# Down weights of a mixture-of-experts stage loaded in runs of 16 KB, with h turned by quarter products

## The chip, the core and the metric

The kernel runs on one core of one Trainium2 chip. Its time is device time in microseconds, from three runs; beside it one execution was recorded by the hardware profiler, and all rows below come from that one. TensorE (PE) multiplies, VectorE (DVE), ScalarE (ACT) and GpSimd (POOL) do the rest, SyncE (SP) issues most of the DMAs, and 16 DMA engines move them.

## The reference

One decoder layer on 576 tokens of 1024 numbers (512 of a prompt, 64 of a sample group): a projection, sparse attention, a pooling branch, a merge, and then a mixture of 32 experts of which each token uses two. All is f32. The change lies in what an expert does, which in the reference is

```python
def run_block(args):
    tok, wt, e = args
    xb = xt[tok]
    hb = jax.nn.silu(xb @ w_exp_gate[e]) * (xb @ w_exp_up[e])
    return (hb @ w_exp_down[e]) * wt[:, None].astype(xb.dtype)
```

with gate and up weights of 1024 x 512 and down weights of 512 x 1024 for each expert, 2 MB each, 6 MB per expert and 201 MB for all 32.

## The kernel before, in words

The program is written by hand, engine by engine: each engine has its own list of instructions, and semaphores tie them together. There is no scheduler; the order on an engine is the order of the code. The layer up to the router takes the first half of the span. Then come the experts, each with a block of 64 token slots (CAP), and at the end the results are gathered and added per token. A second pass for experts with more than 64 tokens stands behind a branch on a flag.

There are two sets of buffers, s = 0 and 1, for even and odd experts; each holds gate (wg), up (wu) and down (wd) weights, 16 KB per partition each. `M[s]` holds the semaphores of a set. For expert n of a set:

- SP issues gate and up of the next expert of the set when the gate product has read them (`gu_done`), and down when the down product is done (`y_done`). All loads are on one queue and are moved in the order of issue. In a partition of wg and wu lie 8 rows of the weights that follow each other in memory, so a partition is one run of 16 KB. In a partition of wd lie 4 rows in two pairs (`by_half`): rows 2p and 2p+1, and rows 256+2p and 256+2p+1, two runs of 8 KB.
- PE multiplies x with gate and up (`gate_up`, 16 products of 512 columns, the two halves of the columns to the PSUM rows 0 to 63 and 64 to 127). Then it turns the x of the other set's next expert (`turn_x`), turns h (`turn_h`) and multiplies it with the down weights (`down`, 8 products of 512 columns).
- ACT applies silu to the gate half (line 1313), copies the turned x (1309) and the turned h (1317) to SBUF. DVE multiplies silu by up into hb (1647) and copies the result out (1651). POOL scatters y and gathers x by indirect DMAs on a queue of its own.

hb has the 64 tokens twice over the partitions: partitions 0 to 63 hold columns 0 to 255 of h and partitions 64 to 127 hold columns 256 to 511. The contraction of the down product runs over partitions, so h must be turned to match the rows of wd: a transpose of all 128 partitions at columns t, t+2, t+4, ... gives for each partition p the rows 2p+t (from the lower half) and 256+2p+t (from the upper half), each for 64 tokens. Two such transposes (t = 0 and 1) give all four.

The first experts are loaded in another order (lines 505 to 529): some weights lie in buffers of their own (wg2, wu2), so that much is in place before PE gets there. For the last expert gate and up come in two halves each (line 539).

Of the kernel before, what the change touches and what calls it, by code (L numbers as in the profile page):

```python
# [13 lines left out]
P = 128  # L14
# [20 lines left out]
NE = EG * EPG  # L35
DE = D // 2
KE = DE // P
CAP = 64
# [86 lines left out]
def program(nc, consts, where, x_prompt, x_sample, cache_k, cache_v, cache_idx_k, state_pool, page_table,  # L125
# [24 lines left out]
    with ctx:  # L150
# [9 lines left out]
        def at(off, *dims, rows=P):  # L160
            n = int(np.prod(dims))
            assert off + n <= AW, (off, dims)
            v = arena[0:rows, off:off + n]
            if len(dims) == 2:
                return v.rearrange("p (a b) -> p a b", b=dims[1])
            if len(dims) == 3:
                return v.rearrange("p (a b c) -> p a b c", b=dims[1], c=dims[2])
            return v
# [5 lines left out]
        def bank(b, n=512, rows=slice(0, P), at0=0):  # L174
            return psum[rows, b * 512 + at0:b * 512 + at0 + n]
# [27 lines left out]
        o = SMALL  # L203
# [23 lines left out]
        o = ZA + P * 9  # L227
# [6 lines left out]
        o = ZA  # L234
# [3 lines left out]
        o = PR  # L238
# [3 lines left out]
        o = PR  # L242
# [4 lines left out]
        o = ZB  # L247
# [32 lines left out]
        o = SMALL  # L280
# [3 lines left out]
        o = GAR + 4 * NT  # L284
# [19 lines left out]
        o = SG + 128  # L304
# [5 lines left out]
        o = SG  # L310
# [3 lines left out]
        xT = [at(o + s * 512, KD // 2, P) for s in range(2)]; o += 1024  # L314
        sg = [at(o + s * 512, DE // 2) for s in range(2)]; o += 1024
        hb = [at(o + s * 512, DE // 2) for s in range(2)]; o += 1024
        hT = [at(o + s * 256, KE // 2, P) for s in range(2)]; o += 512
        yo = [at(W1 - D + s * 512, 512) for s in range(2)]
        onehot = at(SG + 128 + 4 * D, TILES, 2, CAP)
        assert TILES * 2 * CAP <= D and 2 * CAP == P  # L320
# [9 lines left out]
        wd = [at(b + 8192, KE, D) for b in (W0, W1)]  # L330
# [12 lines left out]
        ident = const("ident")  # L343
# [26 lines left out]
        M = [{n: sem(f"{n}{s}") for n in  # L370
              ("wg_in wu_in wd_in xg_in xt_done xt_ev gu_done silu h_ready "
               "ht_done ht_ev y_done y_ev y_st").split()} for s in range(2)]

        OV, N0 = M[0], NE // 2
# [46 lines left out]
        def _(sp):  # L421
# [59 lines left out]

            g_v = w_exp_gate[0].rearrange("e (p k) n -> e p (k n)", k=KD)
            u_v = w_exp_up[0].rearrange("e (p k) n -> e p (k n)", k=KD)
            d_v = w_exp_down[0].rearrange("e (q p t) n -> e p q (t n)", q=2, t=KE // 2)

            def flat(t):
                return t.rearrange("p k n -> p (k n)")

            def by_half(t):
                return t.rearrange("p (q t) n -> p q (t n)", q=2)  # L490

            def load_expert(i, s, first=False, gate=True, up=True):
                e = 2 * i + s
                m = M[s]
                if up and not first:
                    sp.wait_ge(m["gu_done"], i)
                if gate:
                    sp.dma_start(flat(wg[s]), g_v[bass.ds(e, 1), :, :].squeeze(0)).then_inc(m["wg_in"], 16)
                if up:
                    sp.dma_start(flat(wu[s]), u_v[bass.ds(e, 1), :, :].squeeze(0)).then_inc(m["wu_in"], 16)  # L500
                if not first:
                    sp.wait_ge(m["y_done"], i)
                sp.dma_start(by_half(wd[s]), d_v[bass.ds(e, 1), :, :].squeeze(0)).then_inc(m["wd_in"], 16)

            load_expert(0, 0, first=True)
            load_ring(8)
# [6 lines left out]
            sp.dma_start(flat(wu[1]), u_v[1]).then_inc(M[1]["wu_in"], 16)  # L513
            sp.wait_ge(s_xst[0], 48)
            sp.wait_ge(s_xst[1], 32)
            sp.dma_start(by_half(wd[1]), d_v[1]).then_inc(M[1]["wd_in"], 16)
            sp.wait_ge(M[1]["xg_in"], 16)
            sp.dma_start(flat(wu2[0]), u_v[2, :, 0:4 * DE]).then_inc(S["part_in"], 16)
            sp.dma_start(flat(wu2[1]), u_v[2, :, 4 * DE:]).then_inc(M[0]["wu_in"], 16)
# [18 lines left out]
                for w, v, name in zip((wg[1], wu[1]), (g_v, u_v), names):  # L538
                    sp.dma_start(flat(w[:, ks, :]), v[NE - 1, :, 4 * half * DE:4 * (half + 1) * DE]).then_inc((M[1] if half else S)[name], 16)
            sp.wait_ge(M[1]["y_done"], NE // 2 - 1)  # L540
            sp.dma_start(by_half(wd[1]), d_v[NE - 1]).then_inc(M[1]["wd_in"], 16)

            sp.wait_ge(S["flag_ready"], 1)
            over = sp.value_load(flag[0:1, 0:1], min_val=0, max_val=NT)
            with sp.If(over > CAP):
                with sp.Fori(0, NE) as e:
                    sp.wait_ge(OV["y_done"], e * NB + N0)
                    sp.dma_start(flat(wg[0]), g_v[bass.ds(e, 1), :, :].squeeze(0)).then_inc(OV["wg_in"], 16)
                    sp.dma_start(flat(wu[0]), u_v[bass.ds(e, 1), :, :].squeeze(0)).then_inc(OV["wu_in"], 16)
                    sp.dma_start(by_half(wd[0]), d_v[bass.ds(e, 1), :, :].squeeze(0)).then_inc(OV["wd_in"], 16)  # L550
            with sp.Else():
                sp.nop()
            for i in range(TILES):
# [8 lines left out]
        def _(pe):  # L562
# [64 lines left out]
            for k in range(KD):  # L627
                last = pe.matmul(bank(6, HD), xnT[:, k, 0:P], wqi[:, k, NI * HD:NI * HD + HD], start=(k == 0), stop=(k == KD - 1))
# [158 lines left out]
            for u in range(U + 2):  # L787
                if u < U:
                    i, k = units[u]
# [232 lines left out]
            def turn_h(m, s, n):  # L1022
                pe.wait_ge(m["h_ready"], n + 1)
                pe.sem_inc(S["passed"], 1)
                for t in range(KE // 2):
                    last = pe.transpose(bank(1, P, at0=t * P), hb[s][:, t:KE // 2 * (P - 1) + t + 1:KE // 2], ident)  # L1026
                last.then_inc(m["ht_done"], 1)

            def down(m, s, n):
                pe.wait_ge(m["ht_ev"], n + 1)  # L1030
                for k in range(KE):
                    for half in range(2):
                        last = pe.matmul(bank(4 + s, 512, slice(64 * half, 64 * half + 64)), hT[s][:, k % 2, CAP * (k // 2):CAP * (k // 2) + CAP],  # L1033
                                         wd[s][:, k, 512 * half:512 * half + 512],
                                         start=(k == 0), stop=(k == KE - 1))
                last.then_inc(m["y_done"], 1)
# [900 lines left out]
```

## Time and profile before

| | us |
|---|---|
| median of three timed runs | 1116.12 (1114.67 to 1117.65) |
| the profiled execution | 1115.16 |
| its span, first to last instruction | 1113.5 |
| PE busy | 944.4 (85%) |
| mean granted clock of TensorE | 0.951 |
| gate and up products, line 1018 | 238.9 busy, 992 instructions |
| down products, line 1033 | 116.9 busy, 512 instructions |
| a down load, issue to landing | 22.9 (median of 32) |

Slices are fortieths of the span, 27.8 us each. PEclk is the clock granted to TensorE, as a share of 2.4 GHz; 0.50 is 1.2 GHz. PE's busy time is not work at its peak: its instructions overlap, so the time from the first start to the last end of a group says more than their mean. The DMA share is the busy share of the 16 engines; as packets of an engine overlap a little, it can stand slightly above 1. "issue" in the chain is a piece in which the engine waited for nothing that the profile names.

### The profile page before, as it was taken

To read this page: it belongs to the slowest core of one execution; us is meant where nothing else is said; L and a number is where in the kernel's file an instruction comes from. 1 tells how busy PE (TensorE), PEld (TensorE's weight loads), DVE (VectorE), ACT (ScalarE), POOL (GpSimd) and SP (SyncE) were. 2 spreads that over 40 slices of the span, in tenths; PEclk is the share of its full clock that TensorE was granted. 3 is DMA by queue.
4 is the path that set the end of the run, shared out by engine and by line. 5 is a ranking of instruction groups with operands and counts; after the bars stand their busy time and mean duration, and the time that the engine had idled before them with its cause. 6 is when DMAs were issued, how large, how long until landed. Compare 5 with 4: busy or idle time off the path is not lost.

```text
span 1113.5 us, 11556 instructions
## 1 busy us (share of the span) xinstructions
PE 944.4 (85%) x4412; PEld 510.2 (46%) x4412; DVE 338.7 (30%) x743; ACT 201.7 (18%) x445; POOL 198.3 (18%) x296
## 2 busy tenths in 40 slices
PE   7978999999999998999976998788778887887770
PEld 6633444767776566774543433333233333333220
DVE  2269999973331111330143100000000000000006
ACT  3243111213344233000121000000000000000012
POOL 2730650100001200000231121111110111011113
PEclk9989999999999999999996999999999999899995
DMA  9920221610204527913035999999999999999937
GB/s 335 392 78 1 76 85 38 231 39 38 76 1 152 203 100 216 378 64 150 38 126 227 408 419 426 421 424 425 426 423 424 424 425 425 421 425 425 422 136 252
DMA packets 51814, 283.72 MB, mean 255 GB/s; under 512 B 8476, under 2 KB 9344, under 8 KB 32823
## 3 DMA queue, kind: packets, MB, share of 16 engines
q1 hardware_dynamic: 40935, 246.21, 55.0%
q0 software_dynamic: 10784, 36.97, 9.2%
q8 instruction: 25, 0.41, 0.2%
q14 instruction: 14, 0.11, 0.0%
q10 hardware_dynamic: 56, 0.01, 0.0%
HBM read 267.38 MB, written 23.17 MB: 261 GB/s over the span
## 4 chain that ended last, share of the span: by engine, by line
PE 64%; DVE 18%; issue 7%; ACT 4%; DMA 3%; SPq 2%; POOL 1%; ACTq 0%; POOLq 0%; DVEq 0%
PE psum L1018 21%; PE psum L1033 11%; PE psum L780 9%; DVE arena L1421 6%; DVE arena L1419 6%; PE psum L934 5%; PE psum L916 3%; PE psum L604 3%; DMA arena<-in_w_branch_pool 2%; PE psum L1026 1%; PE psum L868 1%; DVE arena L1647 1%; ACT arena L1313 1%; ACT arena L1317 1%; PE psum L834 1%
## 5 line engine op out<-in xcount | busy, mean ns | idle before, releaser
L1018 PE MATMUL psum<-arena 128*64 128x512 f32 x992 | 238.9, 637 | 56.5 <-issue 55.6
L1018 PEld LDWEIGHTS psum<-arena 128*64 128x64 f32 x992 | 86.2, 147 | 207.5 <-issue 207.5
L1033 PE MATMUL psum<-arena 128*64 128x512 f32 x512 | 116.9, 597 | 17.7 <-ACT arena L1317 17.7
L780 PE MATMUL psum<-arena 128*128 128x288 f32 x480 | 126.1, 416 | 0.0
L780 PEld LDWEIGHTS psum<-arena 128*128 128x128 f32 x480 | 89.6, 192 | 31.0 <-issue 8.1
L1647 DVE TENSOR_TENSOR arena<-arena,psum 128x256 f32<-128x256 f32 x32 | 13.5, 421 | 292.1 <-ACT arena L1313 292.1
L1313 ACT ACTIVATE arena<-psum 128x256 f32<-128x256 f32 x32 | 12.3, 384 | 418.1 <-PE psum L1018 407.3
L590 PE MATMUL psum<-arena 128*128 128x512 f32 x192 | 86.2, 604 | 2.1 <-ACT arena L1184 2.1
L1033 PEld LDWEIGHTS psum<-arena 128*64 128x64 f32 x512 | 40.4, 136 | 72.1 <-issue 72.1
L1651 DVE COPY arena<-psum 128x512 f32<-128x512 f32 x32 | 22.1, 691 | 157.1 <-PE psum L1033 157.1
L916 PE MATMUL psum<-arena 128*128 128x288 f32 x256 | 64.3, 415 | 3.7 <-DMA arena<-in_w_branch_pool 3.7
L1419 DVE MAX8 arena<-arena 64x8 f32<-64x1032 f32 (+3 forms) x80 | 66.2, 828 | 2.8
L1845 POOL CAST arena<-arena 128x1 int32 x30 | 5.6, 185 | 329.7 <-DVE arena L1651 329.7
L1421 DVE MATCH_REPLACE8 arena<-arena 64x1032 f32<-64x1032 f32 (+3 forms) x76 | 61.9, 814 | 0.0
L916 PEld LDWEIGHTS psum<-arena 128*128 128x128 f32 x256 | 49.5, 194 | 18.5 <-DMA arena<-in_w_branch_pool 4.6
L590 PEld LDWEIGHTS psum<-arena 128*128 128x128 f32 x192 | 36.3, 193 | 45.1 <-issue 42.8
L934 PE MATMUL psum<-arena 128*128 128x512 f32 x128 | 55.8, 593 | 1.1 <-issue 1.1
L1091 ACT COPY arena<-psum 128x512 f32<-128x512 f32 (+6 forms) x106 | 47.0, 490 | 53.8 <-PE psum L807 31.8
L1701 POOL DMA_INDIRECT arena<-xn_d,arena x32 | 33.4, 1043 | 33.8 <-POOL arena L1839 25.9
L1705 POOL DMA_INDIRECT y_d<-arena x32 | 33.2, 1037 | 29.0 <-POOL arena L1845 27.4
L934 PEld LDWEIGHTS psum<-arena 128*128 128x128 f32 x128 | 23.9, 190 | 29.7 <-issue 29.7
L1821 POOL TENSOR_TENSOR arena<-arena 128x1024 f32<-128x1024 f32 (+1 forms) x5 | 11.7, 2344 | 139.0 <-ACT arena L1301 139.0
(263 smaller groups left out, 930.8 us busy)
## 6 DMA issues: line engine op xcount, KB each, us to landing
arena<-in_w_exp_down SPq DMA_DIRECT2D x32, 2048.0 KB, 22.9
arena<-in_w_exp_gate SPq DMA_DIRECT2D x31, 2048.0 KB, 18.2
arena<-in_w_exp_up SPq DMA_DIRECT2D x30, 2048.0 KB, 22.6
arena<-in_w_in SPq DMA_DIRECT2D x7, 2048.0 KB, 8.6
y_d<-arena SPq DMA_DIRECT2D x1, 8192.0 KB
arena<-in_x_prompt SPq DMA_DIRECT2D x8, 512.0 KB, 7.2
arena<-in_w_out SPq DMA_DIRECT2D x2, 2048.0 KB, 10.4
arena<-in_w_exp_up SPq DMA_DIRECT2D x4, 1024.0 KB, 12.8
```

Of the source, the lines that this page charges most:

```text
L590: last = pe.matmul(bank(b, n, slice(0, r)), lhs, w[:, k, 0:n], start=(k == 0), stop=(k == KD - 1))
L604: last = pe.matmul(out, lhs, wqi[:, k, QIH * half:QIH * half + QIH], start=(k == 0), stop=(k == KD - 1))
L780: last = pe.matmul(bank(2 + n % 2 if n < SAMPLE_G else 2, HN), ring[slot % 2][:, k, m * P:(m + 1) * P], xnT[:, k, HN * hh:HN * hh + HN], s ...
L916: last = pe.matmul(bank(b, HN), w[:, 4 * br + k, m * P:(m + 1) * P], src[:, k, tc], start=(k == 0), stop=(k == 3))
L934: last = pe.matmul(bank(4 + 2 * (i % 2) + half), sgA[k][:, i * P:(i + 1) * P], ring[(R_OUT + half) % 2][:, k, :], start=(k == 0), stop=(k ...
L1018: last = pe.matmul(bank(2 + s, 512, rows).rearrange("p (w n) -> p w n", w=2), x_k, wgu[s][:, :, DE * k + 256 * q:DE * k + 256 * q + 256], ...
L1033: last = pe.matmul(bank(4 + s, 512, slice(64 * half, 64 * half + 64)), hT[s][:, k % 2, CAP * (k // 2):CAP * (k // 2) + CAP], wd[s][:, k, 5 ...
L1091: last = act.copy(out, src(b))
L1419: link(dve.max(m8, src))
L1421: link(dve.match_replace(w, m8, src, LOW))
L1701: pool.indirect_dma_start(xg[s], None, xn2_d, bass.IndirectOffsetOnAxis(ap=sidx[s], axis=0), bounds_check=2 * NT - 1, oob_is_err=False).th ...
L1705: pool.indirect_dma_start(y_halves, bass.IndirectOffsetOnAxis(ap=syid[s], axis=0), yo[s], None, bounds_check=2 * FIRST - 1, oob_is_err=Fal ...
```

## The change

The down weights are loaded as `wg` and `wu` are: partition p gets rows 4p to 4p+3, one run of 16 KB. For h to match, partition p of the turned h must hold columns 4p to 4p+3. Partitions 0 to 63 of it come from the lower half of hb alone and partitions 64 to 127 from the upper half alone, so for each of the four t there are two products with a 64x64 part of the identity: the lower quarter of the array for the lower half, and the upper for the upper. They are plain f32 products in place of transposes, all into bank 1. `hT` has the same size, ordered by t. ACT's copy and the number of down products stay.

```diff
--- before.py
+++ after.py
@@ -314,7 +314,7 @@
         xT = [at(o + s * 512, KD // 2, P) for s in range(2)]; o += 1024
         sg = [at(o + s * 512, DE // 2) for s in range(2)]; o += 1024
         hb = [at(o + s * 512, DE // 2) for s in range(2)]; o += 1024
-        hT = [at(o + s * 256, KE // 2, P) for s in range(2)]; o += 512
+        hT = [at(o + s * 256, KE, CAP) for s in range(2)]; o += 512
         yo = [at(W1 - D + s * 512, 512) for s in range(2)]
         onehot = at(SG + 128 + 4 * D, TILES, 2, CAP)
         assert TILES * 2 * CAP <= D and 2 * CAP == P
@@ -481,13 +481,10 @@
 
             g_v = w_exp_gate[0].rearrange("e (p k) n -> e p (k n)", k=KD)
             u_v = w_exp_up[0].rearrange("e (p k) n -> e p (k n)", k=KD)
-            d_v = w_exp_down[0].rearrange("e (q p t) n -> e p q (t n)", q=2, t=KE // 2)
+            d_v = w_exp_down[0].rearrange("e (p t) n -> e p (t n)", t=KE)
 
             def flat(t):
                 return t.rearrange("p k n -> p (k n)")
-
-            def by_half(t):
-                return t.rearrange("p (q t) n -> p q (t n)", q=2)
 
             def load_expert(i, s, first=False, gate=True, up=True):
                 e = 2 * i + s
@@ -500,7 +497,7 @@
                     sp.dma_start(flat(wu[s]), u_v[bass.ds(e, 1), :, :].squeeze(0)).then_inc(m["wu_in"], 16)
                 if not first:
                     sp.wait_ge(m["y_done"], i)
-                sp.dma_start(by_half(wd[s]), d_v[bass.ds(e, 1), :, :].squeeze(0)).then_inc(m["wd_in"], 16)
+                sp.dma_start(flat(wd[s]), d_v[bass.ds(e, 1), :, :].squeeze(0)).then_inc(m["wd_in"], 16)
 
             load_expert(0, 0, first=True)
             load_ring(8)
@@ -513,7 +510,7 @@
             sp.dma_start(flat(wu[1]), u_v[1]).then_inc(M[1]["wu_in"], 16)
             sp.wait_ge(s_xst[0], 48)
             sp.wait_ge(s_xst[1], 32)
-            sp.dma_start(by_half(wd[1]), d_v[1]).then_inc(M[1]["wd_in"], 16)
+            sp.dma_start(flat(wd[1]), d_v[1]).then_inc(M[1]["wd_in"], 16)
             sp.wait_ge(M[1]["xg_in"], 16)
             sp.dma_start(flat(wu2[0]), u_v[2, :, 0:4 * DE]).then_inc(S["part_in"], 16)
             sp.dma_start(flat(wu2[1]), u_v[2, :, 4 * DE:]).then_inc(M[0]["wu_in"], 16)
@@ -538,7 +535,7 @@
                 for w, v, name in zip((wg[1], wu[1]), (g_v, u_v), names):
                     sp.dma_start(flat(w[:, ks, :]), v[NE - 1, :, 4 * half * DE:4 * (half + 1) * DE]).then_inc((M[1] if half else S)[name], 16)
             sp.wait_ge(M[1]["y_done"], NE // 2 - 1)
-            sp.dma_start(by_half(wd[1]), d_v[NE - 1]).then_inc(M[1]["wd_in"], 16)
+            sp.dma_start(flat(wd[1]), d_v[NE - 1]).then_inc(M[1]["wd_in"], 16)
 
             sp.wait_ge(S["flag_ready"], 1)
             over = sp.value_load(flag[0:1, 0:1], min_val=0, max_val=NT)
@@ -547,7 +544,7 @@
                     sp.wait_ge(OV["y_done"], e * NB + N0)
                     sp.dma_start(flat(wg[0]), g_v[bass.ds(e, 1), :, :].squeeze(0)).then_inc(OV["wg_in"], 16)
                     sp.dma_start(flat(wu[0]), u_v[bass.ds(e, 1), :, :].squeeze(0)).then_inc(OV["wu_in"], 16)
-                    sp.dma_start(by_half(wd[0]), d_v[bass.ds(e, 1), :, :].squeeze(0)).then_inc(OV["wd_in"], 16)
+                    sp.dma_start(flat(wd[0]), d_v[bass.ds(e, 1), :, :].squeeze(0)).then_inc(OV["wd_in"], 16)
             with sp.Else():
                 sp.nop()
             for i in range(TILES):
@@ -1022,15 +1019,17 @@
             def turn_h(m, s, n):
                 pe.wait_ge(m["h_ready"], n + 1)
                 pe.sem_inc(S["passed"], 1)
-                for t in range(KE // 2):
-                    last = pe.transpose(bank(1, P, at0=t * P), hb[s][:, t:KE // 2 * (P - 1) + t + 1:KE // 2], ident)
+                for t in range(KE):
+                    for q in range(2):
+                        rows = slice(CAP * q, CAP * q + CAP)
+                        last = pe.matmul(bank(1, CAP, rows, t * CAP), hb[s][rows, t:KE * (CAP - 1) + t + 1:KE], ident[rows, rows], start=True, stop=True)
                 last.then_inc(m["ht_done"], 1)
 
             def down(m, s, n):
                 pe.wait_ge(m["ht_ev"], n + 1)
                 for k in range(KE):
                     for half in range(2):
-                        last = pe.matmul(bank(4 + s, 512, slice(64 * half, 64 * half + 64)), hT[s][:, k % 2, CAP * (k // 2):CAP * (k // 2) + CAP],
+                        last = pe.matmul(bank(4 + s, 512, slice(64 * half, 64 * half + 64)), hT[s][:, k, :],
                                          wd[s][:, k, 512 * half:512 * half + 512],
                                          start=(k == 0), stop=(k == KE - 1))
                 last.then_inc(m["y_done"], 1)
```

The order of instructions on PE does not change, only what stands in a turn. At the end of the program, in the last pair of experts (the rows are the gate product, the turn of x, the turn of h, the down product, and for the last expert the same without a turn of x), before:

```order
L1018 MATMUL psum<-arena 64x512 x16
L1001 MATMUL psum<-arena 128x128 x4
L1026 MATMUL psum<-arena 128x128 x2
L1033 MATMUL psum<-arena 64x512 x8
L1018 MATMUL psum<-arena 64x512 x16
L1026 MATMUL psum<-arena 128x128 x2
L1033 MATMUL psum<-arena 64x512 x8
```

and in the changed kernel, at the same place:

```order
L1015 MATMUL psum<-arena 64x512 x16
L998 MATMUL psum<-arena 128x128 x4
L1025 MATMUL psum<-arena 64x64 x8
L1032 MATMUL psum<-arena 64x512 x8
L1015 MATMUL psum<-arena 64x512 x16
L1025 MATMUL psum<-arena 64x64 x8
L1032 MATMUL psum<-arena 64x512 x8
```

Two products of 128x128 are now eight of 64x64 between the same neighbours. On SP, at the start of the expert stage (up of expert 2 in two halves, gate of 4, down of 2, up of 4, gate and up of 3, down of 3 and 4), before:

```order
L518 DMA arena<-in_w_exp_up 128x2048
L519 DMA arena<-in_w_exp_up 128x2048
L523 DMA arena<-in_w_exp_gate 128x4096
L503 DMA arena<-in_w_exp_down 128x2x2048
L526 DMA arena<-in_w_exp_up 128x4096
L498 DMA arena<-in_w_exp_gate 128x4096
L500 DMA arena<-in_w_exp_up 128x4096
L503 DMA arena<-in_w_exp_down 128x2x2048 x2
```

and now:

```order
L515 DMA arena<-in_w_exp_up 128x2048
L516 DMA arena<-in_w_exp_up 128x2048
L520 DMA arena<-in_w_exp_gate 128x4096
L500 DMA arena<-in_w_exp_down 128x4096
L523 DMA arena<-in_w_exp_up 128x4096
L495 DMA arena<-in_w_exp_gate 128x4096
L497 DMA arena<-in_w_exp_up 128x4096
L500 DMA arena<-in_w_exp_down 128x4096 x2
```

No load has moved; each down load has one run per partition where it had two.

## Rows read from the trace of the kernel before

**Rows 1.** The page: what the DMA engines moved in 40 slices, and SP's queue.
```profile
GB/s 335 392 78 1 76 85 38 231 39 38 76 1 152 203 100 216 378 64 150 38 126 227 408 419 426 421 424 425 426 423 424 424 425 425 421 425 425 422 136 252
...
q1 hardware_dynamic: 40935, 246.21, 55.0%
```

**Rows 2.** Windows: us, busy PE PEld DVE ACT POOL, clock, DMA share, GB/s.
```profile
600.00:640.00 40.00, 37.24 (x200) 18.08 (x198) 3.34 (x6) 4.03 (x9) 5.29 (x10) 0.97 0.87 356
1000.00:1040.00 40.00, 30.34 (x134) 11.62 (x132) 2.91 (x5) 2.69 (x6) 7.39 (x12) 0.96 1.02 427
```

**Rows 3.** The chain that ended last: start us, us, what.
```profile
637.66 6.88 PE psum L1018 x32
...
675.36 6.88 PE psum L1018 x32
...
687.92 2.65 issue
690.58 8.80 PE psum L1018 x32
...
1050.30 2.67 issue
1052.97 8.69 PE psum L1018 x32
1063.69 3.65 PE psum L1033 x16
1067.34 6.88 PE psum L1018 x32
```

**Rows 4.** Issue to landing of up(30), down(4), gate(4) and down(1), in this order.
```profile
DMA to landing us min/median/max: 23.7/23.7/23.7
...
DMA to landing us min/median/max: 10.8/10.8/10.8
...
DMA to landing us min/median/max: 8.7/8.7/8.7
...
DMA to landing us min/median/max: 7.4/7.4/7.4
```

**Rows 5.** SP's queue, windows 502:506, 585.5:589, 609.2:612.8: packets, MB, share of 16 engines.
```profile
q1 hardware_dynamic: 775, 1.59, 103.0%
...
q1 hardware_dynamic: 182, 1.49, 101.2%
...
q1 hardware_dynamic: 94, 1.54, 99.7%
```

**Rows 6.** The chain again, ahead of the branch products.
```profile
447.32 21.12 DMA arena<-in_w_branch_pool
```

**Rows 7.** Timeline of PE, an expert's turn of h: start us, us, instructions.
```profile
1015.11 0.48 PE L1026 MATMUL psum<-arena 128*128 128x128 f32 x2 [0.34 <-DVE arena L1647]
```

**Rows 8.** Timeline of PE, small f32 products earlier in the program.
```profile
27.37 2.00 PE L616 MATMUL psum<-arena 64*128 64x64 f32 x16
...
330.03 1.09 PE L818 MATMUL psum<-arena 128*64 128x128 f32 x16
...
332.07 1.97 PE L818 MATMUL psum<-arena 128*64 128x128 f32 x32
```

**Rows 9.** The chain, products of 512 columns on the full width.
```profile
529.45 6.87 PE psum L934 x16
```

**Rows 10.** Timeline of SP, and one window, at the start of the experts.
```profile
612.49 0.38 SPq L503 DMA_DIRECT2D arena<-in_w_exp_down  x1
...
625.05 13.01 SPq L503 DMA_DIRECT2D arena<-in_w_exp_down  x2
644.55 0.34 SPq L498 DMA_DIRECT2D arena<-in_w_exp_gate  x1
...
613.00:614.00 1.00, 1.00 (x7) 0.37 (x5) 0.19 (x1) 0.00 (x0) 0.19 (x1) 1.00 0.56 131
```

**Rows 11.** Window at the start of expert 30's gate product; columns as in rows 2.
```profile
1053.00:1056.00 3.00, 3.00 (x8) 1.05 (x10) 0.00 (x0) 0.00 (x0) 0.41 (x1) 0.50 1.02 423
```

## The prediction

> **What bounds the kernel now.** I read the page first, then the windows by stretch, the chain, SP's queue, and last the few places where PE turns a tile. On the page the reader is to see that the core moves 419 to 426 GB/s in slices 24 to 38 [rows 1]: this is the stage of the 32 experts, from 597 to 1080 us, and the change touches nothing else. The windows say what that means: from 1000 to 1040 us the DMA share is 1.02 while PE is busy for 30.3 of 40 us; from 600 to 640 PE is busy for 37.2 and DMA stands at 0.87 [rows 2]. The chain shows the two regimes that follow. Experts 3 to 6 start 12.57 us apart (637.66 to 675.36, three steps) with nothing idle before them; experts 7 to 30 start 15.76 us apart (690.58 to 1052.97, 23 steps), most of them after a piece called "issue", a wait for weights, of 1.3 to 3.3 us; the first of these and the last are shown [rows 3]. So PE works off a lead, and then the loads set the pace. The last such wait stands before expert 30. Its up weights were issued at 1029.2 and landed 23.7 us later [rows 4], at 1052.9, and the gate and up products start at 1052.97 [rows 3]. From there to 1080 PE works without a wait for a load: two turns of h and two down products lie in that stretch. The end of the program is the landing of up(30), plus PE's tail, plus 33 us of combining that stay as they are.
>
> **The down loads.** A down load was 256 runs of 8 KB and becomes 128 runs of 16 KB, as gate and up have, so each of 16 engines handles 8 packets fewer per expert. What does a packet cost beside its bytes? In 4.0 us in which only 2 KB packets move, 775 of them carry 1.59 MB, 397 GB/s, or 82.5 ns each on 16 engines; in 3.5 us of down load alone, 182 packets of 8 KB carry 1.49 MB, 426 GB/s, 307.7 ns each [rows 5]. The 6144 B between them cost 225.2 ns, so 2048 B cost 75.1, and 7.4 ns are left for the packet. Eight packets: 0.059 us per expert. That counts where the down load stands ahead of one that is waited for: down(2) to down(29), 28 loads in the full queue ahead of up(30), and down(0), which SP issues ahead of the branch weights on which the chain waits until 468.5 [rows 6]. 29 x 0.059 = 1.7 us less. Above it stands the packets' own time: 182 packets fill 101.2% of 3.5 us, 311.4 ns each, 94 packets of 16 KB fill 99.7% of 3.6 us, 610.9 ns each [rows 5]; twice the first less the second is 11.9 ns, and 29 x 8 x 11.9 ns = 2.8 us. The rates of the same two windows, 426 and 428 GB/s, give only 0.7 us, and the overhead may be hidden altogether. Below nothing: started on an empty queue, gate(4) in 16 KB runs took 8.7 us to land and down(1) in 8 KB runs 7.4 [rows 4]; if long runs start slower, down(2), the only one near an empty queue, loses up to 1.3 us once. I take 1.7, which lies in the middle and rests on two pure windows of wall time.
>
> The Trainium skill (DMA: Bandwidth & Descriptors, section Why small descriptors are slow) gives a packet a fixed overhead of about 3 cycles beside one per 32 bytes. By that a down load would gain 0.6% of its 4.92 us, 0.8 us over 29 loads where my rows give 1.7, and the sum below would be +1.0 instead of +0.1. The rates 426 and 428 fit that rule better; the 2 KB window fits it worse.
>
> **The turn of h.** Two transposes of 128x128 stand there now, 0.48 us from first start to last end [rows 7]. In their place come eight products. They are f32 products and no transposes, and each f32 product shows as two instructions (the 8 calls at line 1033 are 16 in a row), so 16 instructions with 64x64 stationary and 64 moving columns. No such row exists. Nearest is line 818, 64 stationary and 128 moving columns: 16 instructions in 1.09 us, 32 in 1.97, 0.055 us each [rows 8]. I take 1.09 us, that is D = +0.61 us per expert. From above: line 616, 64 moving columns under 128 stationary ones, 16 in 2.00 us, D = +1.5 [rows 8]. From below: two column halves do run beside each other, as 16 instructions of 512 columns take 3.65 us at line 1033 and 6.87 at line 934 over the full width [rows 3, 9]; if the two quarters of a slice did the same, 16 would take 0.27 + 15 x 0.0275 = 0.68 us, D = +0.2. ACT copies the same 128x256 as before, and the down products again read 64 columns in a row.
>
> **Where D counts.** (a) In the tail, for experts 30 and 31: 2D = +1.2 us. Expert 31's weights bring no new wait, since there is none now (1063.69 + 3.65 = 1067.34 [rows 3]) and PE only gets later. (b) At the start: SP issues down(2) when expert 0's down product is done, at 612.49, with up(4) behind it; the queue had run dry, 131 GB/s from 613 to 614 [rows 10]. The whole D = +0.6 us goes on the load chain. (c) A little later gate(5) is issued at 644.55 by the gate product of expert 3, three turns down the chain; down(4), ahead of it, was issued at 637.69, the second of the two in the row at 625.05, and landed 10.8 us later, at 648.5 [rows 4, 10]. A load needs some 2 us from issue to full rate (the 131 GB/s stand 0.5 to 1.5 us behind down(2)), so there are 3.9 - 2 = 1.9 us of room against 3D - D = 2D = 1.2: enough, up to D = 0.95. (d) In experts 7 to 29 D lies in the wait of 1.3 to 3.3 us for weights. That cover is gone if D passes 15.76 - 12.57 = 3.2 us.
>
> **The sum.** +0.6 (opening) +1.2 (tail) -1.7 (loads) = +0.1 us. The profiled execution took 1115.16 us around its span of 1113.5, so it would be 1115.3; the three timed runs have a median of 1116.12, 0.96 more, and I forecast 1116.2 us. Less than 0.3%, or 3.3 us, can't be told from no change here.
>
> **Rivals.**
> *R1, the packets hide.* Nothing comes back from longer runs and only 3D is left: +1.8 us, 1117.9. For it: 426 and 428 GB/s. Against it: 397 with 2 KB packets, and 311.4 ns twice against 610.9 once [rows 5].
> *R2, faster by the clock.* Expert 30's products came after 2.67 us of idle with the granted clock at 0.50 for their first 3 us, 1.2 GHz, and took 8.69 us where expert 31's took 6.88 at full clock [rows 3, 11]. Over experts 7 to 30, all five waits of 1.3 to 1.9 us were followed by 7.1 us, and of the fifteen of 2.6 us or more ten by 8.4 to 10.0. The change makes PE busier, so that the wait before expert 30 shrinks by some 0.7 to 2.0 us. If the clock then stays at 2.4 GHz, the tail is 1.8 us shorter: 1114.4; with D = 0.2 and 2.8 for the loads it is 1112.1. Against it: a wait between 1.9 and 2.6 us never occurs, so no row tells which way it goes.
> *R3, slower: the quarters don't overlap and the array drains between them.* Both write bank 1, one from rows 0 to 63 and one from rows 64 to 127; where the kernel now has products from both row halves (line 712), they go to two banks. At line 616's 2.00 us D is 1.5: 3 x 1.5, plus 2 x 1.5 - 1.9 = 1.1 us of dry queue at gate(5), less 1.7 = +3.9 us, 1120.0. The opening decides from D = 0.95. If each of the 16 ran its whole 0.28 us alone, D would be 4.0, past the 3.2 of cover: PE would be the bound, 32 x 16.6 us where the stage takes 483, +47 us.
> The Trainium skill (TensorEngine Tiling, Restrictions and Gotchas) says that different row tiles can't access one PSUM bank at the same time, and under Key Properties that a change of tiling mode drains the engine. By that rule something of R3 must come; no row of before has two row tiles on one bank.
> *R4, the change doesn't do what it says*: the runs are cut to 8 KB all the same, +1.8 us. Gate loads do move in 16 KB packets, 94 for 1.54 MB [rows 5], which speaks against it.
>
> **Chances.** Forecast 0.50 (0.46 within 0.3%, 0.02 faster, 0.02 slower); R1 0.16 (0.14 within, 0.02 slower); R2 0.18 (0.14 faster, 0.04 within, as it needs help from D or the loads to pass 3.3 us); R3 0.12 (slower); R4 0.04 (within). Faster 0.16, same 0.68, slower 0.16. The forecast's own range is 1114 to 1118.5; with R1, R2 and the near form of R3 it becomes 1112.0 to 1120.5.
>
> **What would show it.** Queue q1 should carry 4096 packets fewer than 40935 [rows 1]. Each turn should hold 16 instructions in 1.1 us. The waits before experts 7 to 29 should be shorter by about 0.7 us and their spacing 15.70 us (15.76 if R1 holds). down(2) should be issued 0.6 us later. From 1052.97 to the last down product there are 27.0 us; there should be 28.2, or 26.4 at full clock. I am wrong if the spacing moves by more than 0.15 us either way, if the turn takes over 1.5 us, or if the queue runs dry after 640.

## The result and the profile after

| | before | changed |
|---|---|---|
| median of 20 runs, us | 1115.45 (1114.18 to 1117.84) | 1118.45 (1114.0 to 1124.31) |
| ratio to before | | 1.0024 (1.0015 to 1.0033) |
| span of the profiled execution | 1113.5 | 1115.6 |
| SP's queue, packets | 40935 | 36839 |

The changed kernel is 0.24% slower, 2.7 us by the ratio (3.0 by the medians): below the 0.3% that was called "the same" and inside the range, though 0.05 us from the upper end of the forecast's own range of 1114 to 1118.5. It is off the forecast of +0.1 us and clear of noise with this many runs.

The page of the changed kernel shows that the change does what it says: 4096 packets fewer on SP's queue for the same bytes [rows 1], and 512 small instructions, 16 per expert (8 products, each shown as two).

```profile
GB/s 328 390 85 0 76 59 62 207 49 52 76 1 148 195 112 204 370 82 151 38 123 211 404 399 427 425 424 427 427 425 427 427 425 428 424 427 427 422 140 249
...
q1 hardware_dynamic: 36839, 246.21, 54.8%
...
L1025 PE MATMUL psum<-arena 64*64 64x64 f32 x512 | 37.5, 284 | 11.7 <-DVE arena L1646 11.7
```

In the full part of the stage it moves 424 to 428 GB/s where 421 to 426 stood. The chain of the changed kernel (start, us, what) answers to [rows 3]:

```profile
599.19 9.85 PE psum L1015 x32
...
709.89 7.10 PE psum L1015 x32
...
1052.89 1.88 issue
1054.77 7.10 PE psum L1015 x32
1064.60 3.65 PE psum L1032 x16
1068.25 6.88 PE psum L1015 x32
1077.87 3.67 PE psum L1032 x16
```

Expert 8 starts at 709.89 and expert 30 at 1054.77, 22 steps of 15.68 us. In before expert 30 starts at 1052.97 [rows 3] and expert 8 at 706.05 (the row below), steps of 15.77 us:

```profile
706.05 7.10 PE psum L1018 x32
```

So the loads did get faster, by 0.09 us per expert in this pair of traces. One turn, in the timeline of PE (before: [rows 7]):

```profile
1017.38 1.17 PE L1025 MATMUL psum<-arena 64*64 64x64 f32 x16 [0.34 <-DVE arena L1646]
```

With the copy behind it that shifts the down product by 0.70 us (from the start of the turn to the start of the down product it is 1.73 us, and 1.03 before). The prediction had put this D, the extra time of a turn, at 0.61.

The span of one execution can't carry a verdict of 2 us. Expert 0's gate product starts at 599.19 here and at 597.03 before, and in the twelve further traces below it starts anywhere from 596.07 to 599.98, although nothing ahead of it differs in a way that goes with that. And expert 0's gate product itself takes 8.5 to 9.9 us by how soon the clock comes up. I therefore read three numbers from every trace: **M**, from the end of expert 0's gate product to the start of expert 30's; **G**, expert 30's gate product (7.10 us at full clock, 8.5 to 8.8 where it starts at half of it); and **T**, from the start of that product to the end of the last down product, without G.

| kernel | M | G | T |
|---|---|---|---|
| before | 446.28 | 8.69 | 18.27 |
| changed | 445.73 | 7.10 | 19.67 |

M is 0.55 us shorter and T 1.40 us longer, which gives +0.9 us. G is 1.6 us shorter, which would turn the sum to -0.7. The timing says +2.7, so one trace of each doesn't account for the time.

How far can one trace be trusted? M is fixed by the loads and by the turns in the opening. Three kernels of this document have the loads and the opening of before: their M is 446.28, 446.04 and 446.32. Three traces have those of the changed kernel, one of them with the products of the turn in another form: 445.73, 445.60 and 446.09. So M scatters by 0.3 to 0.5 us, and the changed kernel is 0.4 us shorter in the mean (445.81 against 446.21). T repeats to 0.02 us, but for the clock of the last down product. G is partly chance and partly the change itself, as the section on the clock shows.

The last row is one of the prediction's own signs of being wrong. In the windows of the changed kernel (us; busy PE, PEld, DVE, ACT, POOL; clock, DMA share, GB/s) the queue runs dry behind 640 us:

```profile
649.00:651.00 2.00, 1.66 (x20) 1.50 (x20) 0.42 (x1) 0.97 (x2) 0.00 (x0) 1.00 0.81 221
```

Before, at the same distance from expert 0's gate product:

```profile
646.70:648.70 2.00, 2.00 (x10) 0.76 (x11) 0.00 (x0) 0.00 (x0) 0.00 (x0) 1.00 1.01 428
```

### The profile page after: what moved, and what is told of

Its sections match the earlier page's. It is cut to its first block, busy times and chain, and to the rows that moved or that the text cites. A ratio compares the mean times of both kernels' runs of the same rounds, so it can differ in the third digit from the quotient of the medians.

```text
span 1115.6 us, 12452 instructions
## 1 busy us (share of the span) xinstructions
PE 961.2 (86%) x4860; PEld 534.2 (48%) x4860; DVE 338.9 (30%) x743; ACT 201.7 (18%) x445; POOL 199.3 (18%) x296
## 3 DMA queue, kind: packets, MB, share of 16 engines
q1 hardware_dynamic: 36839, 246.21, 54.8%
## 4 chain that ended last, share of the span: by engine, by line
PE 65%; DVE 18%; issue 6%; ACT 5%; DMA 3%; SPq 2%; POOL 0%; ACTq 0%; POOLq 0%; DVEq 0%
PE psum L1015 21%; PE psum L1032 10%; PE psum L777 9%; DVE arena L1420 6%; DVE arena L1418 6%; PE psum L931 5%; PE psum L1025 3%; PE psum L913 3%; PE psum L601 3%; DMA arena<-in_w_branch_pool 2%; PE psum L865 1%; DVE arena L1646 1%; ACT arena L1312 1%; ACT arena L1316 1%; PE psum L613 1%
## 5 line engine op out<-in xcount | busy, mean ns | idle before, releaser
L1015 PE MATMUL psum<-arena 128*64 128x512 f32 x992 | 232.3, 622 | 40.4 <-issue 39.6
L1032 PE MATMUL psum<-arena 128*64 128x512 f32 x512 | 116.9, 597 | 17.7 <-ACT arena L1316 17.7
L777 PEld LDWEIGHTS psum<-arena 128*128 128x128 f32 x480 | 89.6, 192 | 31.0 <-issue 8.1
L913 PEld LDWEIGHTS psum<-arena 128*128 128x128 f32 x256 | 49.5, 194 | 19.3 <-DMA arena<-in_w_branch_pool 5.4
L587 PEld LDWEIGHTS psum<-arena 128*128 128x128 f32 x192 | 36.2, 193 | 45.1 <-issue 42.8
L1025 PE MATMUL psum<-arena 64*64 64x64 f32 x512 | 37.5, 284 | 11.7 <-DVE arena L1646 11.7
L1025 PEld LDWEIGHTS psum<-arena 64*64 64x64 f32 x512 | 34.0, 210 | 17.6 <-issue 17.6
```

The costliest lines, as they stand in the source:

```text
L587: last = pe.matmul(bank(b, n, slice(0, r)), lhs, w[:, k, 0:n], start=(k == 0), stop=(k == KD - 1))
L777: last = pe.matmul(bank(2 + n % 2 if n < SAMPLE_G else 2, HN), ring[slot % 2][:, k, m * P:(m + 1) * P], xnT[:, k, HN * hh:HN * hh + HN], s ...
L913: last = pe.matmul(bank(b, HN), w[:, 4 * br + k, m * P:(m + 1) * P], src[:, k, tc], start=(k == 0), stop=(k == 3))
L1015: last = pe.matmul(bank(2 + s, 512, rows).rearrange("p (w n) -> p w n", w=2), x_k, wgu[s][:, :, DE * k + 256 * q:DE * k + 256 * q + 256], ...
L1025: last = pe.matmul(bank(1, CAP, rows, t * CAP), hb[s][rows, t:KE * (CAP - 1) + t + 1:KE], ident[rows, rows], start=True, stop=True)
```

## The experiments

The theory was that the loads gain a little, and that the longer turn costs in the opening and in the tail alone. The rivals: long runs are part of the loss; the turn costs all along the stage; the form of the quarter products is what makes the turn long.

**Each half of the change alone.** `e1_loads_only` has the new loads and the old turn; `e2_turn_only` the old loads and the new turn. They leave out that h must match the rows of wd, so their outputs are not those of the layer, but the amount of work on each engine is. The same holds below wherever the turn changes without the loads. The diff is the part on the turn of the first kernel against the changed one; the second has the same lines the other way, against the kernel before. In both, `hT` and the index of the down product go with the turn.

```diff
-                for t in range(KE):
-                    for q in range(2):
-                        rows = slice(CAP * q, CAP * q + CAP)
-                        last = pe.matmul(bank(1, CAP, rows, t * CAP), hb[s][rows, t:KE * (CAP - 1) + t + 1:KE], ident[rows, rows], start=True, stop=True)
+                for t in range(KE // 2):
+                    last = pe.transpose(bank(1, P, at0=t * P), hb[s][:, t:KE // 2 * (P - 1) + t + 1:KE // 2], ident)
```

> Down loads in 16 KB runs, but h turned by the two old transposes, so h does not match the rows of wd (the down product sums other pairs than the reference). Theory A (loads gain a little, the longer turn costs in opening, dry queue and tail): the load gain stands alone, spacing of experts 15.68 us, about 1.8 us faster than before (ratio 0.998). Rival B (long runs cost somewhere, for example at the start of a burst or for the branch weights, and are part of the loss): not faster than before, ratio 1.000 to 1.002.

> Down loads in 8 KB runs as before, but h turned by the eight quarter products, so h does not match the rows of wd. Theory A: the longer turn (+0.70 us) costs in the opening (0.9), in a dry queue before expert 5's gate load (about 1.2) and in the tail (1.4): +3.5 to +4.5 us, ratio 1.003 to 1.004, spacing of experts in the load-bound part 15.76 us as before. Rival B: +1.5 us or less, since the loads' part of the loss is absent.

Measured: loads alone 0.9982 (0.9968 to 0.9996), 2.0 us faster; turn alone 1.0038 (1.0022 to 1.0054), 4.2 us slower. Both as theory A had them, and rival B is gone: the longer runs gain and are no part of the loss. The spacing of experts 8 to 30 is 15.68 to 15.70 us in all six traces with 16 KB runs in the middle (that of the pairs below, with another gate product, left aside), and 15.75 to 15.78 in the seven with 8 KB runs. In the traces M is 444.25 with the loads alone (-2.0) and 448.49 with the turn alone (+2.2), T is 18.28 and 21.37. The T of the second holds 1.4 us of turns and 1.7 us that nobody had expected: the last down product took 5.37 us for 3.65 (below).

**Where the turn costs.** Old loads throughout; the quarter products stand in some experts only, chosen in `turn_h` by the number n of the pair: one of these three returns, for experts 0 to 3, for 30 and 31, and for 4 to 29 (`overflow` is set only for the second pass, which keeps the old turn).

```diff
+            def quarters(n):
+                return isinstance(n, int) and n in (0, 1) and not overflow[0]
...
+                return isinstance(n, int) and n == NE // 2 - 1 and not overflow[0]
...
+                return not (isinstance(n, int) and n in (0, 1, NE // 2 - 1)) and not overflow[0]
```

> All loads as before; quarter products in experts 0 to 3 only, whose h then does not match wd. Theory A: opening 0.7 to 0.9 us and a dry queue before gate(5) of about 1.2 us, +2 us, ratio 1.0018. Rival F: less than +0.8 us, the loss being spread over all experts.

> All loads as before; quarter products in experts 30 and 31 only, whose h then does not match wd. Theory A: 2 x 0.70 = +1.4 us, ratio 1.0013, all behind the landing of up(30). Rival F: +0.3 us or less.

> All loads as before; quarter products in experts 4 to 29 only, whose h then does not match wd. Theory A: no change (ratio 1.000, within 0.6 us), since PE waits 1.3 to 3.3 us for weights there; the waits shrink by 0.7 us. Rival F: most of the +4.2 us of the kernel with the turn alone shows here, ratio 1.002 or more.

| turn in experts | ratio | M | G | T |
|---|---|---|---|---|
| 0 to 3 | 1.0033 (1.0019 to 1.0047) | 448.51 | 8.80 | 18.27 |
| 30, 31 | 1.0014 (1.0000 to 1.0029) | 446.04 | 8.55 | 19.66 |
| 4 to 29 | 0.9991 (0.9979 to 1.0003) | 446.32 | 7.10 | 18.28 |
| all 32 | 1.0038 (1.0022 to 1.0054) | 448.49 | 7.10 | 21.37 |

The six experts at the ends pay everything, and 26 turns of 0.70 us in the middle pay nothing. M says it well inside its scatter: +2.23 with the turn in experts 0 to 3, +2.21 with it in all, +0.04 with it in 4 to 29. By time the first kernel is 3.7 us slower where theory A had +2, its interval just above it; the trace gives 2.2, and the rest is not explained. The interval of the second kernel holds rival F's +0.3 us too; T, 1.39 longer, decides it. In the middle the wait for weights takes it up. From 695 to 1053 us PE's waits for weights (total, times, longest) were, before:

```profile
PE psum L1018 <- issue: 53.0, 22, 3.3
```

and with the turn in experts 4 to 29:

```profile
PE psum L1019 <- issue: 37.3, 23, 2.5
```

15.7 us less waiting for some 16 us of turns in that window. Rival F is refuted.

**Inside the opening.** The turn in expert 0 only, and in experts 1 and 2 only (one return each).

```diff
+            def quarters(n, s):
+                return isinstance(n, int) and n == 0 and s == 0 and not overflow[0]
...
+                return isinstance(n, int) and 2 * n + s in (1, 2) and not overflow[0]
```

> All loads as before; quarter products in expert 0 only, whose h then does not match wd. Theory A (two separate places in the opening): down(2) is issued 0.70 us later on a dry queue and everything behind it shifts, expert 30's gate product starts 0.7 us later behind expert 0's gate product than before (446.3 us); gate(5) and the queue ahead of it are late alike, so it brings nothing more. Rival G (the whole +2.2 us of the opening comes from down(2)): +2.2 us. In time +0.7 against +2.2 us, which the timing can hardly tell; the trace can.

> All loads as before; quarter products in experts 1 and 2 only, whose h then does not match wd. Theory A: down(2) is issued as before, gate(5) 1.4 us later on a queue that has almost run dry (dip to about 250 GB/s for two us at 40 us behind expert 0's gate product), expert 30 starts 1.3 to 1.5 us later than before. Rival G: down(2) is all, no shift. Rival H (gate(5) has the 1.9 us of room that the prediction gave it from the landing of down(4)): no shift and no dip.

Expert 0 alone: 1.0005 (0.9996 to 1.0014), M = 446.98, +0.70. Experts 1 and 2: 1.0022 (1.0008 to 1.0036), M = 447.22, +0.94. So there are two places, as A had it, though it had put the second at 1.3 to 1.5 us, and H, the 1.9 us of room for gate(5) of the prediction, is wrong. SP's queue in the kernel with the turn in experts 1 and 2 (timeline; the row with x2 holds down(3) and down(4)), and the window behind gate(5):

```profile
613.17 0.38 SPq L504 DMA_DIRECT2D arena<-in_w_exp_down  x1
...
626.44 13.71 SPq L504 DMA_DIRECT2D arena<-in_w_exp_down  x2
646.63 0.34 SPq L499 DMA_DIRECT2D arena<-in_w_exp_gate  x1
```
```profile
647.00:649.00 2.00, 1.11 (x7) 0.63 (x7) 0.42 (x1) 0.98 (x3) 0.00 (x0) 1.00 0.93 260
```

down(2) is issued 5.8 us behind expert 0's gate product, as in before; gate(5) comes 1.4 us later than there, and at once the rate is 260 GB/s for two us.

Why is there no room? A landing is the end of the slowest of 16 engines, and the traces keep the time at which each of the 16 counted its share of down(4) as done. In before the first was done at 646.05, the last at 648.51 (the landing that the prediction used), the mean is 646.98. gate(5) was issued at 644.55, so the first engine was through with everything ahead of it 1.5 us later and the mean one 2.4 us later, where the landing stands 3.9 us behind. Less the prediction's own 2 us of start, 0.4 us of room are left in place of 1.9, and a delay of 1.4 us costs 1.0 by that estimate; 0.94 was measured. With the turn in experts 1 and 2 the mean engine was through 0.9 us behind the issue of gate(5), in the changed kernel 0.5 us (issue at 648.99, mean 649.48), and with the turn in expert 0 alone, which delays the loads and gate(5) alike, it still was 2.25 us.

The sum of both places, 1.64, is 0.6 short of the 2.23 of all four experts. That is little more than the scatter of M, and whether a later load carries it was not taken apart.

**Is it the row halves?** Quarter products over all 128 rows, so that no product uses a row half.

```diff
-                        last = pe.matmul(bank(1, CAP, rows, t * CAP), hb[s][rows, t:KE * (CAP - 1) + t + 1:KE], ident[rows, rows], start=True, stop=True)
+                        last = pe.matmul(bank(1, CAP, rows, t * CAP), hb[s][:, t:KE * (CAP - 1) + t + 1:KE], ident[:, rows], start=True, stop=True)
```

> The changed kernel with each quarter product taken over all 128 rows against 64 columns of the identity (the other half adds zeros), so no product uses a row half of the array. Theory D (the turn takes 1.17 us because 16 instructions each need 0.055 us to load 64 columns): the turn stays at 1.1 to 1.2 us and the time at that of the changed kernel. Rival E (row halves writing one PSUM bank, or a change of tiling, cost time): the turn falls below 1.0 us and the kernel gets 0.5 to 1.5 us faster than the changed one.

Timeline of PE in that kernel:

```profile
620.87 1.17 PE L1025 MATMUL psum<-arena 128*64 128x64 f32 x16 [0.34 <-DVE arena L1646]
```

The same 1.17 us; M = 445.60, T = 19.68; 1.0014 (1.0000 to 1.0028) against before. The timing is too coarse to tell this kernel from the changed one; the rows decide. Two row halves on one bank cost nothing that shows. What is left fits the number of instructions: 16 at 0.055 to 0.06 us, the spacing of line 818 [rows 8]; no run varied that number. The Trainium skill (TensorEngine Tiling, Restrictions and Gotchas) says that different row tiles can't access one PSUM bank at the same time, and under Key Properties that a change of tiling mode drains the engine. Neither shows as time here: the changed kernel goes from tiles of 64x64 to 128x64 between the turn and the down product and this one doesn't, and from the start of the turn to that of the down product it is 1.73 us in both. ACT's copy stands between the two products, so a short drain could hide behind it. Whether the products of the two halves ever run at once was not measured.

**Two transposes and long runs together.** If the gate and up products deal columns 4j and 4j+1 to the lower half and 4j+2 and 4j+3 to the upper one, two transposes of 128x128 give rows 4p to 4p+3 at partition p.

```diff
-                        rows, cut = slice(CAP * q, CAP * q + CAP), slice(256 * q, 256 * q + 256)
...
-                                             wgu[s][:, :, DE * k + 256 * q:DE * k + 256 * q + 256], start=(k == 0), stop=(k == KD - 1))
+                                             wgu[s][:, :, DE * k:DE * k + DE].rearrange("p w (j a b) -> p w j a b", a=2, b=2)[:, :, :, q, :],
+                                             start=(k == 0), stop=(k == KD - 1))
```

> The whole reference, with 16 KB runs and the two old transposes: the gate and up products take columns 4j and 4j+1 for the lower half and 4j+2 and 4j+3 for the upper half, so that two 128x128 transposes give rows 4p to 4p+3 at partition p. Theory A: as e1_loads_only, 1.8 us faster than before, if a moving operand read in pairs of columns is as fast as one read in a row (gate product 6.9 to 7.1 us). Rival C: the strided read slows the gate products; at twice the time per column they take 14 us and the kernel is some 100 us slower.

Measured 0.9994 (0.9979 to 1.0008): not told from before. Timeline of PE:

```profile
710.33 7.42 PE L1022 MATMUL psum<-arena 128*64 128x512 f32 x32 [0.91 <-issue]
...
718.77 0.47 PE L1031 MATMUL psum<-arena 128*128 128x128 f32 x2 [0.34 <-DVE arena L1652]
```

The turn is short again, but reading pairs of columns costs the gate product 0.34 us (7.44 for 7.10 in the chain), nothing like C's factor of two, though above the 7.1 us that theory A needed. It sits at the same expensive places as D did: T is 18.61, 0.34 above the loads alone, and M = 444.90 is 0.65 above, not much more than M's scatter.

**The hybrid.** Since only the ends pay, in this kernel the ends keep the old form. Experts 4 to 29 are as in the changed kernel, 0 to 3, 30 and 31 as before.

```diff
+            def quarters(n):
+                return not (isinstance(n, int) and n in (0, 1, NE // 2 - 1)) and not overflow[0]
...
+                if isinstance(i, int) and i != 2:
+                    sp.dma_start(by_half(wd[s]), d_v[bass.ds(e, 1), :, :].squeeze(0)).then_inc(m["wd_in"], 16)
+                else:
+                    sp.dma_start(flat(wd[s]), d_v4[bass.ds(e, 1), :, :].squeeze(0)).then_inc(m["wd_in"], 16)
```

> The whole reference. Experts 4 to 29 as in the changed kernel (16 KB runs, quarter products), experts 0 to 3, 30 and 31 as before (two runs of 8 KB, two transposes). Theory A (the longer turn costs only in the opening and in the tail, the loads gain 0.08 us per expert): 26 x 0.08 = 2 us faster than before, ratio 0.998; expert 5's gate load is issued as early as before and the queue does not run dry behind 640 us. Rival F (the turn also costs in the load-bound middle, through the clock or in some other way): ratio 0.999 to 1.001.

> The kernel of e5_hybrid once more, beside the changed one on one chip. By its trace (expert 30 starts 1.9 us earlier, tail unchanged) ratio 0.9983 against before; 0.9987 was measured. If 1.0000 or more comes, the gain of e5_hybrid was chance.

> The changed kernel once more. By the parts (loads alone -2.0, turn in opening +2.2 by the trace, tail +1.4) it should be 1.6 us slower than before, ratio 1.0015. If the first timing holds (1.0024, +2.7 us) there is about 1 us that the parts do not give.

| kernel | ratio | M | G | T |
|---|---|---|---|---|
| hybrid, first | 0.9987 (0.9976 to 0.9999) | 444.39 | 7.10 | 18.27 |
| hybrid, again | 0.9978 (0.9969 to 0.9988) | 444.40 | 8.80 | 18.26 |
| changed, again | 1.0010 (0.9998 to 1.0022) | 446.09 | 7.10 | 21.37 |

The hybrid is 1.4 and 2.4 us faster than before, and its M is 1.9 us shorter twice: 26 loads at 0.07 us. The first timing leaves rival F open (0.999 lies in its interval), the second does not. It beats both kernels. The changed kernel came out at +1.1 us this time, after +2.7: the intervals meet between 1.0015 and 1.0022, +1.7 to +2.5 us.

**The clock before expert 30: rival R2.** The prediction's R2 said that a shorter wait for weights would leave the clock at 2.4 GHz. It had no row with a wait between 1.9 and 2.6 us; the later traces have many. Count the gate products of experts 7 to 30 in all traces but that of the pairs (13 traces, 312 products), by the idle time ahead of them:

| wait, us | products | of these in part at half clock (8.4 us or more) |
|---|---|---|
| under 1.9 | 125 | 0 |
| 1.9 to 2.1 | 19 | 6 |
| 2.1 to 2.6 | 82 | 49 |
| 2.6 and more | 86 | 56 |

The longer turn takes 0.7 us out of each wait. Ahead of expert 30 the wait was 2.27 to 2.67 us in five of the seven traces with transposes in expert 29, and all five products ran in part at half clock; in the other two, where expert 29's own product had been the slow one, it was 1.1 us, and both ran at full clock. With quarter products in expert 29 the wait was 2.00 us or less in all seven traces, and one product of the seven ran in part at half clock. The mean granted clock of all timed executions says the same. It is 0.954 to 0.956 in the kernels with quarter products in experts 4 to 29, and 0.949 to 0.952 in those with transposes there. The cleanest pair is before, 0.951, and the kernel whose middle alone was changed, 0.956, whose time came out 1.0 us lower (interval -2.3 to +0.3). So R2's mechanism is real. At 4 of 7 traces and 1.6 us, my estimate of its worth before expert 30 is 0.9 us. The measured time went the other way, so it is outweighed and not absent.

**The clock in the tail.** In the second trace of the changed kernel the last down product is long. Its timeline, and the windows of that product there, in its first trace and in before, each in a fence of its own:

```profile
1073.11 1.17 PE L1025 MATMUL psum<-arena 64*64 64x64 f32 x16 [1.02 <-DVE arena L1646]
1074.84 5.35 PE L1032 MATMUL psum<-arena 128*64 128x512 f32 x16 [0.55 <-ACT arena L1316]
```
```profile
1074.80:1080.20 5.40, 5.35 (x16) 1.79 (x16) 0.00 (x0) 1.49 (x2) 0.00 (x0) 0.68 0.01 3
```
```profile
1077.90:1081.50 3.60, 3.60 (x16) 1.20 (x16) 0.00 (x0) 1.49 (x2) 0.00 (x0) 1.00 0.02 5
```
```profile
1076.20:1079.90 3.70, 3.64 (x16) 1.26 (x16) 0.00 (x0) 1.49 (x2) 0.00 (x0) 1.00 0.00 0
```

The granted clock is 0.68 over it, so most of it ran at 1.2 GHz, and it costs 1.7 us. That is so in 2 of the 5 traces that have quarter products in expert 31 (the turn alone, and this one), and in none of the 9 that have transposes there. Between the end of the last gate product and the last down product PE works in short pieces and waits for ACT and DVE in between; the quarter products make that stretch 0.7 us longer. With 14 traces this is an association (by chance alone 2 of 2 such cases would fall to those five in 1 of 9 draws), no proof. As a mean it would add 0.7 us, about what R2 gives back.

## Why the prediction was right, and where it was off

- *What bounds.* Right. The landing of up(30) plus PE's tail is the end of the program; T moved as the parts said. M did in kind, but the halves don't quite add up: the opening costs 2.2 us of M with the old loads and 1.6 with the new ones (445.81 in the mean, for 444.25 with the loads alone).
- *The loads, -1.7 us.* Right in kind and nearly in size: -2.0 by time and by M. The packet's price from two pure windows, 7.4 ns, was a little low (1.9 us of M over 26 loads of 8 packets fewer is 9 ns); the 11.9 ns from the packets' own times gave 2.8 and was too high. The 0.8 us estimated from the Trainium skill (DMA: Bandwidth & Descriptors, Why small descriptors are slow) are too few. No sign of a slower start.
- *The turn, D = 0.61.* Measured 0.70; line 818's spacing had given 0.61. Both ends of the bound (0.2 and 1.5) missed, and the taken value was near.
- *Term (a), the tail, +1.2 us.* Measured +1.40, twice 0.70, and in some executions 1.7 more by the clock, a term the prediction did not have. Whether the turn brings it about is open.
- *Term (b), expert 0's turn on the load chain, +0.6 us.* Right: +0.70 in M with the turn there alone.
- *Term (c), room behind gate(5): the step that failed.* The prediction took the 3.9 us from the issue of gate(5) to the landing of the load ahead, less 2 us of start, as 1.9 us of room, and put the cost at nothing below D = 0.95. The mean engine was through 2.4 us behind the issue, so the room was 0.4 us, and the experiment with experts 1 and 2 shows +0.94 us of M from a delay of 1.4. The opening cost 1.6 us in the changed kernel and 2.2 with the old loads, in place of 0.6. The prediction's own last sign of being wrong, a queue that runs dry after 640, came true with the 221 GB/s at 649 us; its other two did not (the spacing moved by 0.09 us, the turn takes 1.17).
- *Term (d), the middle costs nothing.* Right, within the scatter of M.
- *The sum.* Forecast +0.6 +1.2 -1.7 = +0.1. By the changed kernel's own traces it is +1.6 +1.4 -2.0 = +1.0. The clock adds some 0.7 behind the last gate product and takes some 0.9 before expert 30 (estimates from few traces). The timings say +2.7, +1.1 and, for the form over full rows, +1.6. The gap to the sum, about 1 us, is open. The chance of "the same" was well placed, since every term was small. That the time fell inside the forecast's own range, by 0.05 us, is luck; the mechanism of the opening was wrong.
- *R2.* Its mechanism is there: in the profiled execution expert 30's products took 7.10 us behind a wait of 1.88 us, and from their start to the last down product there were 26.8 us, near the 26.4 of "full clock" and not the 28.2 of the forecast. The gain at one such place is 1.6 us (8.69 to 7.10); the 1.8 of the prediction compared with a piece of 6.88 that the next group cuts short. The forecast had no term for it.
- *R3.* Its mechanism (row halves on one bank) does not show; its place, gate(5), was the right one at a smaller D than it named.

What stays open: 0.6 us of the opening's 2.2 with the old loads, why the opening costs less with the new ones, about 1 us of the time of the changed kernel, and whether the half clock on the last down product comes from the quarter products.

## What to carry to other kernels

Put a small gain for the loads and a small loss for the engine next to each other only after asking at which places each is on the path: in a stage bound by its loads 26 of 32 longer turns were free, and the six at the ends cost 3.6 us with the old loads, or 3.0 with the new ones, where all the loads gave 2.0. So give the middle of such a stage the form that is best for the loads and the ends the form that is best for the engine. And do not take the landing of the load ahead as the time until which a queue is full: the first of 16 engines was through 2.5 us ahead of it. Look too at what a shorter wait does to TensorE's clock; here it took back some of the loss.

## What the runs showed of the hardware that I had not expected

- At an issue 3.9 us ahead of the landing of the load before it there was little slack: a delay of 1.4 us cost 0.94 us of queue time. The 16 engines finished their shares of that load over 2.5 us (646.05 to 648.51).
- Of 125 gate products behind a wait of less than 1.9 us none ran in part at half clock, of 19 behind 1.9 to 2.1 us six did, and of 168 behind longer waits 105. Taking 0.7 us out of the waits raised the mean granted clock from 0.951 to 0.956.
- A moving operand read in pairs of f32 columns (8 bytes of every 16) takes 7.44 us for 32 instructions of 512 columns, against 7.10 when it is read without gaps: 5%, not a factor of two.
- f32 quarter products take the same 1.17 us for 16 instructions with 64x64 and with 128x64 stationary tiles, two row halves on one PSUM bank included.
- Going from 8 KB to 16 KB runs raised the rate from 700 to 1040 us from 424 to 426 GB/s (hybrid) and took 0.07 to 0.09 us off each 2 MB load that changed (by M and by the spacing of experts).
